# Three edits in a one-core decoder step: the order of the last retention head, the release of a query buffer, and one more low part a quad on VectorE

## The reference

```python
h = rmsnorm(x, norm_mix_g); proj = h @ w_in          # pooling mixer + 4 retention heads
a = pool_mix(p_ext, pos, pool_w, pool_scale)
b, s_new = retention_mixer(q, k, v, gate, pos, s0, ret_norm_g)
x = x + concat([a, b]) @ w_out
x = x + mem_attn(rmsnorm(x, norm_mem_g), mk, mv, w_mq, w_mo)   # 4 heads, 256 memory tokens
x = x + peer(rmsnorm(x, norm_ffn_g), peer_wq, peer_subkeys, peer_u, peer_v)

# retention, one head: o_t = q_t S_t, S_t = gamma S_(t-1) + k_t^T v_t, then
mu = mean(o); var = mean(square(o - mu)); o = (o - mu) * rsqrt(var + eps)
# peer: 8 heads choose 16 of 16384 experts a token
act = gelu(einsum('thkd,td->thk', peer_u[expert], x)); out = einsum('thk,thkd->td', g * act, peer_v[expert])
```

## Time and profile before

| what | value |
|---|---|
| median of 3 runs | 4602.15 us |
| profiled execution | 4598.67 us |
| its span | 4596.9 us |
| PE busy (weight loads) | 4377.5 us, 95% (4138.6 us, 90%) |
| POOL busy | 2814.5 us, 61% |
| DVE busy | 2453.6 us, 53% |
| ACT busy | 1534.4 us, 33% |
| granted TensorE clock, mean | 0.985 |

### The profile page before, as it was taken

How to read it: one execution, slowest core, us unless ns; L and a number is a source line. 1 busy time by engine, 2 the same in 40 slices (tenths; PEclk the granted TensorE clock), 3 DMA queues, 4 the chain that set the end, 5 groups by cost and what they waited for, 6 DMA issues and landing times.

```text
span 4596.9 us, 75376 instructions
## 1 busy us (share of the span) xinstructions
PE 4377.5 (95%) x28747; PEld 4138.6 (90%) x28747; DVE 2453.6 (53%) x3198; ACT 1534.4 (33%) x1928; POOL 2814.5 (61%) x1440
## 2 busy tenths in 40 slices
PE   7999999899999989999999998999999999999997
PEld 6899989799888978888888898999999999999997
DVE  3632333413102155555555865777777777777656
ACT  4422222222222234444443553333333333333333
POOL 6933222243222447777777787787888788886653
PEclk9999999999999999999999999999999999999998
DMA  6643333344554245555656568999999899999853
GB/s 217 201 102 102 108 107 109 107 142 144 193 190 177 82 156 183 183 183 182 183 182 184 163 205 317 364 357 346 355 358 358 311 362 358 356 357 347 316 196 138
DMA packets 491785, 1032.01 MB, mean 225 GB/s; under 512 B 55680, under 2 KB 281088, under 8 KB 458880
## 3 DMA queue, kind: packets, MB, share of 16 engines
q1 hardware_dynamic: 314384, 590.67, 38.8%
q0 software_dynamic: 45056, 268.60, 15.0%
q10 hardware_dynamic: 132208, 170.85, 10.6%
HBM read 935.26 MB, written 94.73 MB: 224 GB/s over the span
## 4 chain that ended last, share of the span: by engine, by line
issue 35%; POOL 28%; PE 25%; DMA 7%; DVE 3%; ACT 2%; POOLq 0%; SPq 0%; ACTq 0%; DVEq 0%
POOL WS L450 25%; PE PS L564 13%; PE PS L939 13%; DMA RAW<-in_vE 6%; POOL AR L474 2%; ACT WS L970 1%; POOL ROWS L484 1%; DVE AR L1550 0%; DVE AR L1844 0%; DVE AR L1576 0%; DMA AR<-gel 0%; DMA pmap<-ROWS 0%; DMA AR<-in_vE,AR 0%; DVE AR L1828 0%; PE PS L906 0%
## 5 line engine op out<-in xcount | busy, mean ns | idle before, releaser
L564 PE MATMUL PS<-HL,WS 128*128 128x288 f32 (+2 forms) x16896 | 2392.9, 303 | 75.0 <-DVE HL L1587 19.7
L564 PEld LDWEIGHTS PS<-HL,WS 128*128 128x128 f32 x16896 | 2348.9, 190 | 97.2 <-issue 45.6
L450 POOL TENSOR_TENSOR WS<-RAW,WS 128x1024 fp32r<-128x1024 f32 x602 | 1477.8, 2466 | 1437.6 <-ACT WS L970 1434.5
L970 ACT ACTIVATE WS<-RAW 128x1024 fp32r<-128x1024 f32 x602 | 616.4, 1055 | 1156.0 <-PE PS L564 436.7
L939 PE MATMUL PS<-WW,WS 128*128 128x320 f32 x6144 | 927.6, 313 | 57.0 <-POOL WS L450 47.9
L939 PEld LDWEIGHTS PS<-WW,WS 128*128 128x128 f32 x6144 | 910.3, 190 | 73.7 <-issue 38.1
L853 PE MATMUL PS<-WS,HL 128*128 128x512 f32 x3072 | 700.7, 390 | 2.9 <-POOL WS L450 2.9
L853 PEld LDWEIGHTS PS<-WS,HL 128*128 128x128 f32 x3072 | 575.8, 188 | 121.8 <-POOL WS L450 3.4
L450 POOL TENSOR_TENSOR WS<-CS,WS 128x1024 fp32r<-128x1024 f32 x200 | 491.2, 2456 | 135.3 <-ACT WS L970 133.3
L1901 DVE SCALAR_TENSOR_TENSOR PS<-ROWS,AR,PS 128x2048 f32<-128x2048 f32 x206 | 483.6, 2347 | 10.2 <-DMA ROWS<-in_vE,AR 9.8
L1916 DVE TENSOR_TENSOR AR<-AR,PS 128x320 f32<-128x320 f32 x512 | 247.6, 484 | 324.1 <-PE PS L939 323.0
(11 more groups left out here) (169 smaller groups left out, 2470.3 us busy)
## 6 DMA issues: line engine op xcount, KB each, us to landing
RAW<-in_uT SPq DMA_DIRECT2D x256, 512.0 KB, 4.7
RAW<-in_w_lin SPq DMA_DIRECT2D x218, 512.0 KB, 3.5
CS<-in_uT SPq DMA_DIRECT2D x128, 512.0 KB
AR<-in_uT SPq DMA_DIRECT2D x128, 512.0 KB
RAW<-in_vE SPq DMA_DIRECT2D x128, 512.0 KB, 6.5
CS<-in_vE SPq DMA_DIRECT2D x64, 512.0 KB
AR<-in_vE SPq DMA_DIRECT2D x64, 512.0 KB
AR<-in_w_lin SPq DMA_DIRECT2D x46, 512.0 KB
```

What stands on the lines that cost most here:

```text
L450: pool.tensor_tensor(WS[:, k, 1, :], raw(k, many, late), WS[:, k, 0, :].bitcast(F32), ALU.subtract)\
L564: ins = mm(to, WS[:, slot + hf, wp, k * P:(k + 1) * P], x, start=first and (wp, xp) == (0, 0), stop=last and wp == 1, skip_group_check=True)
L970: copy = lambda out, in_, **kw: act.activation(out, in_, ACT.Identity, **kw)
```

## The change

**Last retention head.** ACT copies OSR behind input block 2, the outputs behind block 4 and the state behind block 7 (`after` of `split_early`). PE puts the means first, then the first round of states, the variances, the second round; the state rounds use banks 4, 5, 2, 3 in place of 4 to 7. DVE centres OT behind nine low parts and makes the last four sample states behind the variances. Heads 0 to 2 keep their order.

**Query buffer.** ACT loads input blocks 3 to 6 when PE has done the prompt's scores (`qm_free`) and DVE has copied the samples' queries (`qz_done`).

**A fifth low part a quad.** DVE makes the low parts of slots 3, 7, 11, 13 and 15 (in quads 27 to 31 those of 3, 5 and 7). The new one stands behind the sum of d = 4. In quad 0 slot 7's stands earlier.

```diff
+LOW_DVE, LOW_TAIL = (3, 7, 11, 13, 15), (3, 5, 7)
+def by_dve(k, tail=False):
+    return k % 8 in LOW_TAIL if tail else k % 16 in LOW_DVE
...
-                if k % 4 == 3:
-                    sp.wait_ge(S["low_done"], low_uv(i4, k - 4))
+                if by_dve(k - 4, tail):
+                    sp.wait_ge(S["low_done"], low_uv(i, k - 4, tail))
...
-                    if k % 4 < 3:
+                    if not by_dve(k):
                         low_part(H_UV + 16 * i + k // 4 * 4, k % 4, late=True)
...
+                def last_states(k2):
+                    if k2 == 0:
+                        pe.wait_ge(S["o_evac"], h + 1)
+                        pe.wait_ge(S["spr_evac"], h + 1)
+                        means()
+                    elif k2 == 2:
+                        pe.wait_ge(S["km_done"], h + 1)
+                        pe.wait_ge(S["lin_evac"], h * 8 + (B_HEAD + 5 + 3))
+                        state_round(0, LAST_BANKS)
+                    elif k2 == 4:
+                        variances()
+                    elif k2 == 5:
+                        pe.wait_ge(S["sst_new"], h * SB + 4)
+                        state_round(1, LAST_BANKS)
...
-                    out_early(H_OUT, B_OUT, 0, OUT_EARLY, LO_OUT, between=states)
+                    out_early(H_OUT, B_OUT, 0, OUT_EARLY, LO_OUT, between=last_states)
+                    pe.wait_ge(S["sst_new"], h * SB + 8)
...
-                        mm(bank(4, MEM, off=MEM * t), QM[:, c, P * t:P * (t + 1)], KT[:, c, :],
-                           start=c == 0, stop=c == 3, skip_group_check=True)
+                        ins = mm(bank(4, MEM, off=MEM * t), QM[:, c, P * t:P * (t + 1)], KT[:, c, :],
+                                 start=c == 0, stop=c == 3, skip_group_check=True)
+                ins.then_inc(S["qm_free"], 1)
...
-                    split_early(mixT, Z_OUT, OUT_EARLY, (0, 0, 0), LO_OUT)
+                    split_early(mixT, Z_OUT, OUT_EARLY, (0, 0, 0), LO_OUT,
+                                lambda b: copy_samples(h) if b == 2 else copy_outputs(h) if b == 4 else copy_state(h) if b == 7 else None)
...
-                    act.wait_ge(S["ks_used"], h * SB + SB)
+                    act.wait_ge(S["qz_done"], h + 1)
+                    act.wait_ge(S["qm_free"], h + 1)
                     for b in range(3, 7):
                         load_om(b)
...
+                    lows(Z_OUT, LO_OUT, 0, 9)
+                    centred()
+                    lows(Z_OUT, LO_OUT, 9, 11)
+                    new_states(0, LAST_BANKS)
+                    lows(Z_OUT, LO_OUT, 11, OUT_EARLY)
                 dve.wait_ge(S["rvar_done"], h + 1)
                 ts(halves(RVAR), pair(3), EPS, None, ALU.add).then_inc(S["rvar_ready"], 1)
+                if not more:
+                    new_states(1, LAST_BANKS)
...
                 def after(d):
-                    if d in (1, 9):
-                        low_last(H_UV + 16 * i + 11 + d // 2)
+                    if d in (1, 4, 9):
+                        low_weights(H_UV + 16 * i, 11 + d // 2)
```

More of the change, by code:

```diff
@@ L110, in split, with so_far, split_uv, low_uv @@
     return n + 5
-def split_uv(i12, k):
-    assert k % 4 < 3
-    return i12 + (H_UV + 5 + k // 4 * 3 + k % 4)
-def low_uv(i4, k):
-    return i4 + (k // 4 + 2)
+LOW_DVE, LOW_TAIL = (3, 7, 11, 13, 15), (3, 5, 7)
+def by_dve(k, tail=False):
+    return k % 8 in LOW_TAIL if tail else k % 16 in LOW_DVE
+def so_far(i, k, tail, dve, first):
+    n = 8 if tail else 16
+    all_of = [j for j in range(n) if by_dve(j, tail) == dve]
+    main = sum(by_dve(j) == dve for j in range(16)) * QT if tail else 0
+    return i * len(all_of) + (first + main + sum(j <= k % n for j in all_of) - (len(all_of) if k < 0 else 0))
+def split_uv(i, k, tail=False):
+    return so_far(i, k, tail, False, H_UV + 4)
+def low_uv(i, k, tail=False):
+    return so_far(i, k, tail, True, 2)
 class Steps:
@@ L409, in load_quarters, with load_v @@
                                  .rearrange("b p w -> p b w")).then_inc(S[f"raw{k % 4}"], 16)
-            def load_v(i, i12, i4, first):
+            def load_v(quad, i, first, tail=False):
                 for q in range(4):
@@ L513, in _ @@
             with pool.Fori(0, NQ - QT) as i:
-                for k in (0, 1, 2, 4, 5, 6):
+                for k in (j for j in range(8) if not by_dve(j, True)):
                     low_part(i * 8 + (H_V + k // 4 * 4), k % 4, late=True)
@@ L924, in up, with down @@
                     projection(i * 16 + (H_UV + 4 * a + 2 * e), i * 4 + (B_UV + 2 * a + e), e, 2 * e, dense, first_bank=e,
-                               weights=lambda hf: weights_uv(i * 12, i * 4, 4 * a + 2 * e + hf))
-            def down(i12, i4, first, i, W, back=False):
+                               weights=lambda hf: weights_uv(i, 4 * a + 2 * e + hf))
+            def down(first, i, W, back=False, tail=False):
                 pe.wait_ge(S["ww_ready"], i * 4 + 4)
@@ L954, in quad @@
                     up(i, a)
-                down(i * 12, i * 4, 8, i, WW, back)
+                down(8, i, WW, back)
             for c in range(2):
@@ L1024, in split_early @@
                         load(b + 2)
+                    if after:
+                        after(b)
             def split_last(src, early):
@@ L1140, in evac_head, with copy_samples, copy_outputs, copy_state @@
                 high2(h * 16 + (H_HEAD + 2 * m + 4), 2 * (m % 2))
+            def copy_samples(h):
+                act.wait_ge(S["so_done"], h + 1)
+                copy(OSR, bank(6, RD)).then_inc(S["so_copied"], 1)
+            def copy_outputs(h):
+                act.wait_ge(S["o_done"], h * 2 + 1)
+                copy(OT[:, :, 0:TP], PS[:, 2048:3072].rearrange("p (c n) -> p c n", c=2))
+                act.wait_ge(S["so_turned"], h + 1)
+                turned = bank(6, RD, off=RD).rearrange("p (c q x) -> p c q x", c=2, q=4)
+                for r in range(2):
+                    ins = copy(by_token(OT, r), by_group(turned, r))
+                ins.then_inc(S["o_evac"], 1)
+            def copy_state(h):
+                act.wait_ge(S["o_done"], h * 2 + 2)
+                copy(SPR, bank(7).rearrange("p (c n) -> p c n", c=2)).then_inc(S["spr_evac"], 1)
+                act.wait_ge(S["spr_evac"], h + 1)
+                act.dma_start(nret_p[bass.ds(h, 1)].rearrange("a (c p) v -> p (a c) v", p=P), SPR).then_inc(S["out_spr"], 16)
+            def store_states(h, first, end):
+                for b in range(first, end):
+                    act.wait_ge(S["sst_new"], h * SB + (b + 1))
+                    act.dma_start(nret_s[b, bass.ds(h, 1)].rearrange("a (c p) v -> p (a c) v", p=P), SST[:, b])\
+                        .then_inc(S["out_sst"], 16)
             def retention(h, more):
```

125 lines of the change are left out of this document (64 added, 61 removed), and 2 rows, old and new, of the table names.

## The result

The changed kernel took 4630.64 us (median of 6 runs, 4622.77 to 4638.84), the kernel before 4597.32 us (6 runs in turn with it, 4591.28 to 4606.64). The ratio is 1.0073, 95% interval 1.0056 to 1.009: slower by 0.73%. The forecast was 4618 us, with a range of 4578 to 4640, and slower as the likeliest outcome.

A forecast was written before the change was run, and what follows sets the result against it. PE, busy 95% of 4596.9 us, was taken to bound the kernel, so changes pay only where it stands still. 4598.67 - 16.3 - 7 + 42.3 = 4617.7 us, forecast as 4618, range 4578 to 4640.

The forecast's parts named there:

- Edit 3: Quads 1 to 25: DVE waits for slot 13's high part, delaying sums PE needs; 42.3 us slower, bounds 0 to 50.
- The quads of 58.4 and 60.2 us: Sign in the quads: a quad would take about 60.2 us in place of 58.4.
- The clock: PE's clock in the quads: about 9 falls of 0.9 us replace 5 of 1.8, so taken as 0.
- Quad 0: First quad: waits for stores and gathers in the same places, whoever makes the low parts; 0 us.
- Edit 1: Last retention head: earlier copies and transposes let PE restart at 905.0, 16.3 us faster, bounds 10 and 18.
- Edit 2: Last memory head: four input block loads issued at 1393.5, not 1397.19; 7 us faster, bounds 3.6 and 8.
- The last block's low part comes near 1410.4: Last memory head: PE starts the last input block there and not at 1418.16, 7.7 us earlier.
- A: Rival in the quads: the fifth low part helps and the wait on POOL goes; 4546 us, chance 0.06.
- B: Rival in the quads: slot 13's load lands earlier, so the price a quad is 0; 4576 us, chance 0.10.
- C: Rival in the quads: the clock falls in every quad, 25 falls in place of 5; 4643 us, chance 0.07.
- D: Rival in the last retention head: its reordering gains nothing; 4634 us, chance 0.07.

The follow-up runs named there:

- experiment 4: Changed kernel with slot 13's low part on DVE behind sum d = 6 instead of d = 4: 4572.89 us, ratio 0.9938 to the kernel before.
- experiment 2: Kernel before with only the fifth low part on DVE, head and query buffer as before: 4646.9 us, ratio 1.0099 to the kernel before.
- Experiment 11: Slot 13 behind sum d = 5, rows spread, and quad 0's first four loads given their own slots' counts: 4564.17 us, ratio 0.9916 to the kernel before.
- experiment 5: Changed kernel with slot 13's low part behind sum d = 5 and gathered rows behind sums 2, 7, 10, 12, 14: 4568.83 us, ratio 0.9928.
- experiment 1: Changed kernel without the fifth low part, only the head's new order and early query buffer: 4581.29 us, ratio 0.9955 to the kernel before.
- experiment 9: Changed kernel with each gathered row fetched at half width, 1024 of 2048 elements: 4555.79 us, ratio 0.9897 to the kernel before.
- experiment 3: Kernel before with only the last retention head's new order: 4580.47 us, ratio 0.996 to the kernel before.
- experiment 6: Changed kernel with slot 9 in place of slot 13 as fifth low part on DVE: 4599.1 us, ratio 0.9995 to the kernel before.
- experiment 10: Changed kernel with slots 9 and 13 both on DVE, experiment 5's places, first row behind sum d = 3: 4600.05 us, ratio 0.9993.
- experiment 7: Experiment 1's kernel plus three spare 256-element SBUF subtractions on DVE behind sum d = 4: 4604.68 us, ratio 1.0001 to the kernel before.

## Why the prediction was right, and where it was not

**Edit 3, the mechanism: right, and shown.** DVE waited 3.3 us a quad in front of the new low part (forecast near 3), PE's wait went from POOL to DVE's sums, and moving that one instruction took the loss away (experiment 4). Its price can be compared without the drift of the loads: a quad ends 11.51 us behind the start of slot 13's high part before (59.25 - 47.74) and 13.20 us after (61.08 - 47.88). The 1.69 us between them, 25 times, are 42.2 us; forecast were 42.3. The trace of experiment 2, with the same third part, gives 13.23 us. The rest of the 45.5 us is slot 13 coming 0.14 us later in the quad. (The quads of 58.4 and 60.2 us among the prediction's signs are not the averages, which were 59.25 and 61.08.)

**The clock: 0 as a net, as forecast, but not by the numbers given.** PE was busy 14.7 us longer on the same matmuls, and idle 30.7 us longer. Where a wait in front of d = 7 is followed by matmuls at the 1.2 GHz level, they fill time in which PE would else have waited for the sum of d = 6, so these 14.7 us don't come on top of the 42.3. The dates show the net: from the start of slot 13's high part to d = 8 a quad takes 1.81 us longer (3.80 before, 5.61 after), and from d = 8 to its end 0.12 us less (7.71, 7.60). The first is 45.1 us in all and not 42.3, the second -3.0 and not 0. In eight quads d = 8 came 2.0 to 2.6 us later, where the forecast had 1.91 at most, and all eight are among those with eleven or more matmuls at the 1.2 GHz level. Such quads went from 5 to 10 (forecast: 5 to about 9).

**Quad 0: costed at nothing, and it cost about 4 us here, 4 to 11 in five traces.** This is the step that failed: "Quad 0 waits for stores and gathers in the same places, whoever makes the low parts". The prediction looked at where quad 0 waits for stores and gathers and not at what the change does to the counts that its first loads wait for. `slot_free(0, k)` asks for the slot four before. With `k - 4` negative, `by_dve(k - 4)` says "slot 13" for slot -3, so the load of slot 1 waits for `low_done`, which DVE first posts when its loop of the stage before is over; and slot -4 gets a count that is one higher than before, so the first load waits for one more period of POOL (6 us). The low parts of slots -4 and -3 are both made by POOL. Experiment 11 gave these loads their own counts, and the loss was gone. The order of instructions shows none of this, since no instruction moves; it has to be computed from the formulas for the first turn.

**Edit 1: right.** The forecast was -16.3; it is -17.2 in this trace and 16.9 on average over eleven. The dates: transposes at 864.89 (866.8 less the 1.7 us by which this execution was ahead is 865.1), reciprocal at 887.99 (888.2), restart at 903.17 (903.3), remaining wait 3.58 us (4).

**Edit 2: mis-sized.** The forecast was -7; it is -3.9 in this trace, and -3.0 to -4.8 over the ten. The loads were issued when it said, the fourth block was split when it said (1382.27 and the 18.9 us are 1401.2; forecast 1401.4), and the next three followed without a wait. The step that failed is the one behind them, "The last block's low part comes near 1410.4": it takes the gain at these blocks for the gain at the last one. The five blocks that follow waited for loads of their own, 0.74 to 1.98 us each and 6.0 us in all. The last was split at 1393.59, with the 18.9 us 1412.5, and before at 1416.63: 4.1 us earlier. What held these loads is not shown; eight loads of 512 KB for the memory values run on SP's queue beside them.

**The rivals.** A, that the fifth part helps: not as written. In another place it costs nothing and probably gains (experiments 4, 5 and 11, 8 to 17 us below experiment 1 by the medians). B, that longer quads bring slot 13 earlier: slot 13 came no earlier, 47.9 us after 47.7; the point from which it would decide was real, as experiment 9 shows with 44.2 us. C, the clock falling in every quad: it fell in 10 of 25. D, no gain from the head: experiment 3 rules it out.

Added up from the trace, after minus before: -1.7 us ahead of the head, -17.2 in it, -3.9 in the memory head, +1.0 up to quad 0, +4.1 through quad 0, +45.5 in quads 1 to 25, +0.7 from there to the last high part, +1.0 behind it: +29.5 us, where the prediction had +19.0. Quad 0 makes 4.1 of the difference, edit 2 makes 3.1 and the quads 3.2. Against the median the prediction is 12.6 us low; what is left is within the spread of single runs.

## What to carry to other kernels

Before an instruction is handed to the engine with more free time, ask when its input is there and what is queued behind it: 1.2 us of work that had to wait 3.3 us for its input cost 1.7 us a quad, and the same work two sums later cost nothing. A wait has to be followed to the transfer that dates it: where the transfers fill nearly all of the time (0.90 to 0.93 here), taking an engine's wait away can bring it back at a later load or gather (experiments 6 and 10). And where waits are counted by a formula over a pattern that repeats, work out the first turn by hand: the slots in front of it don't follow the pattern.

## What the runs showed of the hardware that was not expected

A subtraction on VectorE with both inputs in SBUF stands still while GpSimd's subtraction runs. With 256 elements it took 0.42 us alone and 2.03 us beside GpSimd, and all 27 that began during GpSimd's instruction ended 0.28 us behind it (experiment 7); the low part of 1024 elements took 1.23 us on average in the changed kernel and 2.54 us in experiment 9, where it began during GpSimd's. With one input in PSUM, 75 such instructions took 0.42 us on average, and 67 of them began during GpSimd's. The Trainium skill says this in SBUF — State Buffer, Who interferes with whom: an instruction of VectorE with two SBUF inputs contends with one of GpSimd that reads SBUF, and the one that issues second is blocked until the other is done. The trace agrees. It makes a dummy instruction a poor probe unless its inputs lie where they can't collide.
